# Branch A mixed inside the second half of the input projection, its projection in products of 512 columns

## What is computed

```python
h = rms_norm(x, norm_in)
u_a, v_a, z_a, q_b, k_b, v_b, z_b, gate_a, gate_b = jnp.split(h @ w_in, SPLIT_POINTS, axis=-1)
u_a = gelu(u_a)
v_a = rms_norm(gelu(v_a), norm_v)
y_a = u_a * (tril(w_s) mixed over the 128 tokens of a chunk, per group, of v_a + b_s) * silu(z_a)
y_b = stick_breaking_attention(q_b, k_b, v_b) * silu(z_b)
merged = sigmoid(gate_a) * (y_a @ w_o_gmlp) + sigmoid(gate_b) * (y_b @ w_o_sb)
out = rms_norm(x + merged @ w_out, norm_final)
```

## Time and profile before

| | us |
|---|---|
| runs of the kernel | 2737.62, 2732.68, 2734.16 |
| their median | 2734.16 |
| the profiled execution | 2735.23 |
| its span | 2733.5 |
| PE busy | 2588.9 (95%) |
| DVE, ACT, POOL busy | 1597.4, 1260.0, 933.4 |

### The profile page before, as it was taken

How to read it: one execution, slowest core, us unless ns; L and a number is a source line. 1 busy time by engine, 2 the same in 40 slices (tenths; PEclk the granted TensorE clock), 3 DMA queues, 4 the chain that set the end, 5 groups by cost and what they waited for, 6 DMA issues and landing times. The chain is left out here.

```text
span 2733.5 us, 38907 instructions
## 1 busy us (share of the span) xinstructions
PE 2588.9 (95%) x13812; PEld 2225.4 (81%) x13812; DVE 1597.4 (58%) x2057; ACT 1260.0 (46%) x2212; POOL 933.4 (34%) x776
## 2 busy tenths in 40 slices
PE   6999999999989999999995999799999999799998
PEld 5888888888768888888885999678877778689997
DVE  7555555555655455555543444698888899534342
ACT  5664333443454433333432221588888878411111
POOL 3444232232444333232321221466666665000000
PEclk9999999999999999999996999999999999899999
DMA  3333333333322333333336444121221122443331
GB/s 105 103 111 116 116 99 119 100 119 109 95 68 77 108 100 118 107 109 119 100 100 192 139 131 154 70 70 59 77 77 47 72 77 77 139 154 111 120 123 61
DMA packets 239712, 283.57 MB, mean 104 GB/s; under 512 B 12048, under 2 KB 189200, under 8 KB 236560
## 3 DMA queue, kind: packets, MB, share of 16 engines
...
...
## 5 line engine op out<-in xcount | busy, mean ns | idle before, releaser
L722 PE MATMUL in_bank<-in_a_hi,in_w_hi 128*128 128x512 f32 x1988 | 779.3, 392 | 24.9 <-ACT in_o L411 9.4
L724 PE MATMUL in_bank<-in_a_lo,in_w_hi 128*128 128x512 f32 x1988 | 776.4, 391 | 0.0
L725 PE MATMUL in_bank<-in_a_hi,in_w_lo 128*128 128x512 f32 x1988 | 776.2, 390 | 0.0
L722 PEld LDWEIGHTS in_bank<-in_a_hi,in_w_hi 128*128 128x128 f32 x1988 | 374.7, 188 | 106.4 <-ACT in_o L411 10.5
L725 PEld LDWEIGHTS in_bank<-in_a_hi,in_w_lo 128*128 128x128 f32 x1988 | 374.9, 189 | 78.4
L724 PEld LDWEIGHTS in_bank<-in_a_lo,in_w_hi 128*128 128x128 f32 x1988 | 375.2, 189 | 77.4
L567 DVE TENSOR_TENSOR in_w_lo<-carried_buffer,in_w_hi 128x512 fp32r<-128x512 f32 x213 | 245.3, 1152 | 263.9 <-ACT in_w_hi L407 260.9
L407 ACT ACTIVATE in_w_hi<-in_sums 128x512 fp32r<-128x512 f32 x284 | 179.0, 631 | 473.2 <-PE in_bank L725 326.2
L1573 DVE TENSOR_TENSOR_SCAN att_rest<-att_z_ps,att_rest 128x512 f32<-128x512 f32 (+3 forms) x320 | 355.3, 1116 | 47.5 <-ACT att_z_ps L1522 44.8
L1480 POOL TENSOR_TENSOR att_slot<-att_slot,att_rest 128x512 f32<-128x512 f32 (+3 forms) x320 | 304.5, 957 | 216.3 <-DVE att_rest L1573 215.7
L303 POOL TENSOR_TENSOR in_sums<-carried_buffer 128x512 f32<-128x512 f32 x71 | 91.7, 1291 | 704.5 <-DMA carried_buffer<-in_w_in 704.2
...
## 6 DMA issues: line engine op xcount, KB each, us to landing
carried_buffer<-in_w_in SPq DMA_DIRECT2D x144, 512.0 KB, 4.7
uz_T<-in_o SPq DMA_DIRECT2D x32, 256.0 KB, 4.7
va_T<-in_o SPq DMA_DIRECT2D x32, 256.0 KB, 3.3
q_T<-in_o SPq DMA_DIRECT2D x32, 256.0 KB, 3.5
k_T<-in_o SPq DMA_DIRECT2D x32, 256.0 KB, 3.7
vb_T<-in_o SPq DMA_DIRECT2D x32, 256.0 KB, 3.6
zb_T<-in_o SPq DMA_DIRECT2D x32, 256.0 KB, 3.6
ga_T<-in_o SPq DMA_DIRECT2D x32, 256.0 KB, 3.6
```

The source lines that it names most:

```text
L722: pe.matmul(bank[:, :], hi, a_hi[:, i, k], start=opens and k == 0, stop=False, skip_group_check=True)
L724: pe.matmul(bank[:, :], hi, a_lo[:, i, k], start=False, stop=False, skip_group_check=True)
L725: mm = pe.matmul(bank[:, :], lo, a_hi[:, i, k], start=False, stop=k == HALF_K - 1, skip_group_check=True)
```

## The change

1. In pairs 36 to 71 TensorE is visited twice by branch A: after P7 and after P4 (`visit`). Pair 37 loads w_s, b_s, norm_v and the first two va and uz tiles; in pairs 37 and 38 w_s is transposed. Then tile t (128 tokens, 16 in all) is turned in pair 39 + 2t and mixed in pair 40 + 2t. All of it goes through bank 7. The buffers (va, uz, v_raw, w_T, w_scaled, bias) are views of `h_T`, y is `x_sb`.
2. The mixing is one float32 product per group (v_raw with w_scaled), 128x128 each, in place of three float32r ones. 1/rms is not applied to v but to the weights: ACT writes w_scaled = w_T / rms for each tile. Squares are taken by ACT from the bank, in halves of 512; DVE copies v_raw and multiplies by norm_v, also in halves; POOL adds the bias and multiplies by uz. SP stores y as a new intermediate `ya_T`.
3. Stage A (`project_a`) only projects and gates: 4 chunks of 512 tokens, 8 x 8 x 3 matmuls of 512 columns each, eight banks in place of four, ya loaded in halves of 1 MB, gates and results in pieces of 256 KB, all on SP's queue. q, k and vb of head 0 are loaded after the first chunk.
4. TensorE's loop over the second group is written out.

```diff
+    WEIGHTS_AT, MIX_AT = PAIRS + 1, PAIRS + 3
...
+    def turned_in(n):
+        return (n - MIX_AT) // 2 if n >= MIX_AT and (n - MIX_AT) % 2 == 0 and (n - MIX_AT) // 2 < NT else None
+    def mixed_in(n):
+        return turned_in(n - 1)
...
+        place = h_T[:, :, :].rearrange("p k t -> p (k t)").rearrange("p (n e) -> p n e", e=D)
+        va, uz = ([place[:, n].rearrange("p (g t) -> p g t", g=GROUPS) for n in at] for at in ((0, 1), (2, 3)))
+        v_raw, w_T, w_scaled, bias = (place[:, n] for n in range(4, 8))
+        y = [x_sb[:, n] for n in range(2)]
+        mask_in = x_sb[:, 0].rearrange("p (g t) -> p g t", g=GROUPS)
...
+            def load_mix_weights():
+                sp.wait_ge(turned, 4 * TILES)
+                sp.dma_start(mask_in, w_s[0].rearrange("g t s -> t g s")).then_inc(w_s_loaded, 16)
+                for i in range(PRODUCTS_7):
+                    sp.wait_ge(a_ready[i], 2)
...
+            def load_va(t):
...
+                if t >= 2:
+                    sp.wait_ge(v_turned, 2 * (t - 1))
+                sp.dma_start(va[t % 2], va_n[:, :, t * P:(t + 1) * P]).then_inc(va_loaded[t % 2], 16)
+            def load_uz(t):
+                if t >= 2:
+                    sp.wait_ge(y_done, t - 1)
+                sp.dma_start(uz[t % 2], uz_n[:, :, t * P:(t + 1) * P]).then_inc(uz_loaded[t % 2], 16)
+            def store_tile(t):
+                sp.wait_ge(y_done, t + 1)
+                sp.dma_start(ya_n[:, :, t * P:(t + 1) * P], y[t % 2].rearrange("p (g t) -> p g t", g=GROUPS))\
+                    .then_inc(y_stored[t % 2], 16)
...
             def pair(n):
                 t0 = n // PAIRS * GROUP
                 t1 = slice(t0, t0 + CW)
+                if n == WEIGHTS_AT:
+                    load_mix_weights()
+                    for tile in range(2):
+                        load_va(tile)
+                        load_uz(tile)
+                if mixed_in(n) is not None and mixed_in(n) + 2 < NT:
+                    load_va(mixed_in(n) + 2)
+                if mixed_in(n - 1) is not None:
+                    store_tile(mixed_in(n - 1))
+                    if mixed_in(n - 1) + 2 < NT:
+                        load_uz(mixed_in(n - 1) + 2)
...
+            def add_bias(t, half):
+                cols = halves_v[half]
+                pool.wait_ge(gained, 2 * t + half + 1)
+                pool.tensor_tensor(y[t % 2][:, cols], y[t % 2][:, cols], bias[:, cols], ALU.add).then_inc(biased, 1)
+            def times_uz(t):
+                pool.wait_ge(biased, 2 * t + 2)
+                pool.wait_ge(uz_loaded[t % 2], 16 * (t // 2 + 1))
+                pool.tensor_tensor(y[t % 2], y[t % 2], uz[t % 2].rearrange("p g t -> p (g t)"), ALU.mult)\
+                    .then_inc(y_done, 1)
             def pair(n):
+                if mixed_in(n) is not None:
+                    rms_v(mixed_in(n))
                 if n + 1 < LAST:
                     for i in range(4):
                         weight_sum(i, n + 1)
                 if tile_of(n):
                     rms(tile_of(n))
+                if n == WEIGHTS_AT:
+                    pool.wait_ge(w_s_loaded, 16)
+                    pool.affine_select(out=mask_in, in_=mask_in, compare_op=ALU.is_ge, fill=0.0, base=0,
+                                       pattern=[[0, GROUPS], [-1, P]], channel_multiplier=1).then_inc(masked, 1)
+                    pool.wait_ge(bias_loaded, 16)
+                if mixed_in(n) is not None:
+                    add_bias(mixed_in(n), 0)
...
+                if mixed_in(n) is not None:
+                    add_bias(mixed_in(n), 1)
+                    times_uz(mixed_in(n))
...
+            def squares_v(t, half):
+                act.wait_ge(v_kept, 2 * t + half + 1)
+                act.activation(bank_t[:, :], bank_t[:, :], ACT.Square, accum_out=v_sum[:, t, half:half + 1])\
+                    .then_inc(v_squared, 1)
+            def scale_w(t):
+                act.wait_ge(v_rms_done, t + 1)
+                act.wait_ge(w_kept, 2)
+                wait_past(act, mixed, 2 * t)
+                act.activation(w_scaled, w_T, ACT.Copy, scale=v_rms[:, t:t + 1]).then_inc(w_scaled_done, 1)
...
+            def keep_v(t, half):
+                dve.wait_ge(v_turned, 2 * t + half + 1)
+                wait_past(dve, mixed, 2 * t)
+                dve.tensor_copy(v_raw[:, halves_v[half]], bank_t[:, :]).then_inc(v_kept, 1)
...
+            def gain_mix(t, half):
+                dve.wait_ge(mixed, 2 * t + half + 1)
+                dve.wait_ge(gain_v_loaded, 16)
+                if t >= 2:
+                    dve.wait_ge(y_stored[t % 2], 16 * (t // 2))
+                g4 = slice(half * GROUPS // 2, (half + 1) * GROUPS // 2)
+                dve.tensor_tensor(y[t % 2][:, halves_v[half]].rearrange("p (g t) -> p g t", g=GROUPS // 2),
+                                  bank_t[:, :].rearrange("p (g t) -> p g t", g=GROUPS // 2),
+                                  gain_v[:, g4].unsqueeze(2).to_broadcast([P, GROUPS // 2, P]), ALU.mult)\
+                    .then_inc(gained, 1)
+            def visit(n, second):
+                if n in (WEIGHTS_AT, WEIGHTS_AT + 1) and second:
+                    keep_w(n - WEIGHTS_AT)
+                if turned_in(n) is not None:
+                    keep_v(turned_in(n), second)
+                if mixed_in(n) is not None:
+                    gain_mix(mixed_in(n), second)
...
+            def turn_v(t, half):
+                pe.wait_ge(va_loaded[t % 2], 16 * (t // 2 + 1))
+                if half:
+                    pe.wait_ge(v_squared, 2 * t + 1)
+                elif t:
+                    pe.wait_ge(gained, 2 * t)
+                else:
+                    pe.wait_ge(w_kept, 2)
+                for k in range(GROUPS // 2):
+                    ins = pe.transpose(bank_t[:, k * P:(k + 1) * P], va[t % 2][:, half * GROUPS // 2 + k, :], ident[:, :])
+                ins.then_inc(v_turned, 1)
+            def mix(t, half):
+                if half:
+                    pe.wait_ge(gained, 2 * t + 1)
+                else:
+                    pe.wait_ge(v_squared, 2 * t + 2)
+                    pe.wait_ge(w_scaled_done, t + 1)
+                for k in range(GROUPS // 2):
+                    gs = slice((half * GROUPS // 2 + k) * P, (half * GROUPS // 2 + k + 1) * P)
+                    mm = pe.matmul(bank_t[:, k * P:(k + 1) * P], v_raw[:, gs], w_scaled[:, gs], start=True, stop=True)
+                mm.then_inc(mixed, 1)
...
+            def visit(n, second):
+                if n in (WEIGHTS_AT, WEIGHTS_AT + 1) and second:
+                    turn_w(n - WEIGHTS_AT)
+                if turned_in(n) is not None:
+                    turn_v(turned_in(n), second)
+                if mixed_in(n) is not None:
+                    mix(mixed_in(n), second)
...
                 product(P7, bank_b[b], g, n)
+                if g:
+                    visit(n, 0)
                 pe.wait_ge(c12_done, n + 1)
                 product(P5, bank_c[b], g, n)
                 pe.wait_ge(c21_done, n + 1)
                 product(P4, bank_d, g, n)
+                if g:
+                    visit(n, 1)
...
-            with pe.Fori(PAIRS // 2, PAIRS) as t:
-                for b in range(2):
-                    pair(t, b, 1, False)
+            for n in range(PAIRS, LAST):
+                pair(n // 2, n % 2, 1, False)
...
+def project_a(nc, w_o_gmlp, s, carried):
+    ya_k, ga_k, pa_k = (s[n].rearrange("(k p) s -> p k s", p=P) for n in ("ya_T", "ga_T", "pa_T"))
+    N_WO = D // WT
+    HALF = KT // 2
+    with ExitStack() as memory:
+        sc = Scope(nc, memory, "a")
+        wo_in = [*(carried.as_weights(n) for n in range(N_WO - 1)), sc.sb("wo_in", [P, KT, WT])[:, :, :]]
+        wo_hi, wo_lo = (sc.sb(n, [P, KT, D], F32R) for n in ("wo_hi", "wo_lo"))
+        ya_in = sc.sb("ya_in", [P, KT, CW])
+        ya_hi, ya_lo = (sc.sb(n, [P, 2, KT, CW], F32R) for n in ("ya_hi", "ya_lo"))
+        gate = sc.sb("gate", [P, KT, CW])
+        p_ps = [sc.ps(f"p_ps{n}", [P, CW]) for n in range(KT)]
...
+        @block.sync
+        def _(sp):
+            def load_ya(c, half):
+                if c:
+                    sp.wait_ge(ya_lo_done, 2 * (c - 1) + half + 1)
+                sp.dma_start(ya_in[:, rows(half)], ya_k[:, rows(half), tokens(c)]).then_inc(ya_loaded[half], 16)
+            def load_wo(n):
+                sp.dma_start(wo_in[n], w_piece(w_o_gmlp, n)).then_inc(wo_loaded[n], 16)
+            def load_gate(c, k):
+                wait_past(sp, stored[k], 16 * c)
+                sp.dma_start(gate[:, k], ga_k[:, k, tokens(c)]).then_inc(gate_loaded[k], 16)
+            load_ya(0, 0)
+            load_ya(0, 1)
+            for n in range(1, N_WO):
+                load_wo(n)
+            for k in range(KT):
+                load_gate(0, k)
+            for c in range(NC):
+                if c + 1 < NC:
+                    for half in range(2):
+                        load_ya(c + 1, half)
```

(65 more changed lines are left out.)

379 lines of the change are left out of this document (76 added, 303 removed).

## The result

| | before | after |
|---|---|---|
| median of the runs, us | 2734.8 | 2692.6 |
| lowest to highest | 2732.7 to 2737.6 | 2692.4 to 2693.7 |
| profiled execution / its span | 2735.2 / 2733.5 | 2692.4 / 2690.5 |

The ratio is 0.9846, with a 95% interval of 0.9829 to 0.9863: 42 us or 1.5% faster. The forecast was 2711.6, the range 2690 to 2742. The sign and the range held; the saving was nearly twice the forecast's 23.6 us.

The account below looks back on a forecast made before the run. It took TensorE to bound the input projection's second half and stage A's body. 2735.2 - 88.6 saved in stage A + 65.0 added to the input projection (16.5 + 43.5 + 2 + 3) = 2711.6 us; range 2690 to 2742.

Parts of the forecast that it names:

- A: Whole kernel: the forecast itself, 2711.6 us, reaching from 2705 to 2719 by stage A's start and the waits; chance 0.53.
- C: Input projection: a float32 mixing product costs a 512-column stream, 0.227 us, 29.1 in all, total 2697; chance 0.12.
- Stage A: Gate and project stage, last input product to attention's first: 201.7 us where it was 290.3, saving 88.6.
- Start: Beginning of stage A: its first product comes 17.3 us after the last input product.
- Tail: End of stage A: 8.0 us from its last product's start to attention's first, 9.75 before.
- rival E: Stage A: ya halves or weight pieces stall each of four chunks for 3 us, 12 us, total 2724; chance 0.06.
- Transposes: Input projection, pairs 37 to 71: 16 tiles and w_s at 0.97 us each add 16.5 us of TensorE work.
- The mixing product: Input projection: 128 float32 products at 0.34 us, the price of the three float32r ones replaced, add 43.5 us.
- Rival B: Input projection: a float32 mixing product costs four passes like four 128-column products, 0.45 us; +14.5, total 2726; chance 0.15.
- Waits: Input projection: 2 us for late weights in pair 37, and 3 us for SP's queue at 0.2 us a tile.
- Rival D: Input projection: tile transfers make weights late in every pair, 2.5 us a tile, 40 us added, total 2749; chance 0.14.
- My slack of 1.0 us: Input projection pair: u2, released by the weights' landing and rounding, is done 1.0 us before TensorE needs it for P7.

Follow-up runs that it names:

- mix_wide: Changed kernel with each of the 128 float32 mixing products streaming 512 columns of w_scaled instead of 128: 2772.6 us against 2692.6.
- near_after: Changed kernel with the tile transfers (va; ya and uz) issued right after the load of the weights in SP's queue: 2728.7 us against 2692.6.
- near_before: Changed kernel with the tile transfers (va; ya and uz) issued right before the load of the weights in SP's queue: 2699.0 us against 2692.6.
- mix_twice: Changed kernel with each block of float32 mixing products issued twice, 128 products more: 2719.9 us against 2692.6.
- mix_r3: Changed kernel with each float32 mixing product replaced by three float32r products of 128x128, the mixing itself left out: 2705.7 us against 2692.6.
- mix_r1: Changed kernel with each float32 mixing product replaced by one float32r product of 128x128, the mixing itself left out: 2680.0 us against 2692.6.

## Why the prediction was right, and where it was off

By its own steps, on the profiled executions: forecast -23.6, measured 2735.2 - 2692.4 = -42.8. The sign held because stage A's saving, the larger term, was right to about 1 us. The scenario did not: A, given 0.53, reached from 2705 to 2719, and what came was C, given 0.12. That the result still lies in the range is owed to its lower end, 2.6 us below the result; C without waits adds up to 2692, not to the 2690 that the prediction gives it.

- **Stage A**: forecast 201.7 us, measured 200.6. Start 16.4 for 17.3 (the first half of ya landed 5.1 us after its issue, not 6.5; ACT and DVE 1.9 and 2.3 as taken). From the first product to the last 176.2: 767 spacings of 0.2267 are 173.9, and the ten at half clock cost 2.1 (2.3 forecast). Tail 8.1 for 8.0. No chunk stalled, so rival E is out. Gain 89.7 for 88.6.
- **Transposes**: 17 x 8 x 0.111 = 15.1 us by the blocks, 16.5 forecast.
- **The mixing product is the term that failed.** 43.5 us forecast (0.34 each), 28.7 measured (128 x 0.224): 14.8 of the 19.2 us by which the forecast was too high. I took the price of three float32r products, "since its row has the same tile shape and is the middle of the upper part", a choice: no row said that a float32 product costs as much. The value is rival C's, 0.227, whose total of 2697 was the nearest of all; its reason (the stream of 512 columns) is what mix_wide supports, since 4 x 128 columns are 512. Rival B had the passes right and their price wrong (mix_wide, by the growth per column), and my own argument against it ("128 columns four times is no more stream than one of 512") should have carried the weight: the product costs 0.224 us, one stream of 512 columns 0.2267.
- **Waits**: 5 us forecast (2 in pair 37, 3 for late weights). The input projection grew by 47.6; less 15.1 and 28.7 are 3.8, of which 0.8 lie ahead of pair 36's o11 and 1.8 are added waits of TensorE for u2 (3.8 us by the weight loads, 2.0 before); 1.2 are not placed. The size was near, but by luck: the 3 us were for weights held up by transfers issued behind them, and such transfers take next to nothing from them (near_after: 3.6 and 5.3 us, 3.6 and 5.0 without).
- **Rival D** did not come, and for reasons that I had not given. At the head of the pair the tile's transfers stand behind the weights and behind the store of o12, and are gone before the next weights; and the visits give the weights time. Put right ahead of the weights (near_before) they do make them late, by 1.6 to 1.8 us, and that costs 6.4 us, not 40. The 36 us of near_after are near D's 40 by chance: there the transfers are issued 16 us later than in this kernel (at 1164 in place of 1148.7 in the pair shown), behind the weights, and it is the store of o12 that is late. My slack of 1.0 us was right, but it was the store's as much as the weights'; the prediction looked at the weights alone.
- The rest of the program after attention's first product was 0.7 us shorter. With 14.8 + 1.4 + 1.2 + 1.1 + 0.7 the 19.2 us close. They are read from one execution of each kernel, and the end of the input projection alone moves by up to 4 us between executions, so only the 14.8, which mix_twice, mix_r3 and mix_r1 bear out by runs, is sure; the small terms are not.
